# Layer kernel of a diffusion block on one core: token parts for the last two groups of the down projection, loads and splits of two earlier groups moved

## The chip, the core and the metric

One core of a Trainium2 chip runs the whole kernel. The metric is the device time in microseconds (us), the median of several executions. Engines: PE is TensorE (matrix products), DVE is VectorE, ACT is ScalarE, POOL is GpSimd, SP is SyncE, which here only issues transfers. POOL issues transfers too, on a queue of its own.

## What is computed

```python
x = x + g1 * mix
x = x + g2 * _swiglu(_modulate(_rms_norm(x, norm2_g[l]), sh2, sc2), w_ffn_in[l], w_ffn_out[l])
...
return _rms_norm(x, norm_f_g)

def _swiglu(u, w_ffn_in, w_ffn_out):
    gate, up = jnp.split(u @ w_ffn_in, 2, axis=-1)
    return (jax.nn.silu(gate) * up) @ w_ffn_out
```

There are 512 tokens (T) of 2048 features (D); the hidden layer has 5632 features. The change touches only the product with `w_ffn_out` (the down projection) and the final norm. One more number matters: the last 1024 columns of the adaptive modulation (`c @ w_ada`) is computed beside the down projection, in 16 "pieces" of 128 x 1024 weights.

## The kernel before

Every tile has features on the 128 partitions and tokens along the row. Float32 products are made of three fp32r products: high part of the weights by high part of the data, high by low, low by high. ACT makes a high part (a copy to fp32r), DVE the low part (a subtraction), and PE then multiplies.

**The down projection** has two kinds of work. The first 16 rows of 128 hidden features and all outputs are done in *the block*: eight periods (p = 64 to 71, `NALL` to `NEND` - 1) of seven products each, in the order A11, S2, S1, A22, A12, S3, S4; the count `product_done` tells how many are finished. The other 28 rows are done in *groups* of four rows: `NG` = 7 groups for each of three passes over the outputs, 21 in all, numbered gg = 0 to 20 (`LAST` = 20). Groups 0 to 6 run ahead of the block, 7 to 13 and 14 to 20 behind it. A group has one hidden tile (1 MB) and three units of weights (512 KB each; two units in the last pass). A unit is 24 matmuls of 512 tokens (L1805 to L1816), so a group of three units is 72 matmuls, one of two units 48. `SETS` gives each group one of three sets of buffers.

**Who does what for a group.** SP loads it (`group`, `hidden`, `down` in L627 to L643; buffers `hb_f` for the hidden tile and `bw_f` for a unit), waiting until the last group with the same buffers is used. ACT makes the high parts `hb_h` and `bw_h`, DVE the low parts `hb_l` and `bw_l` (`prep(gg)`: the hidden tile first, then the units in turn; PE can start once the first unit's low part is there). Each engine runs its list strictly in order, so the order written in the code decides what waits behind what.

**The pieces.** POOL loads piece n into one of four buffers, once DVE has used piece n - 4 (`pool.wait_ge(ada2_used, n - 3)`). DVE accumulates them (`late(first, end)`, L1947 and L1950, tile `ada_al`). ACT waits for the sixteenth before it splits token sums for the block (L1307), behind `prep(5)`.

**Behind the block.** POOL adds the block's results to `x1_feature_major` in device memory, two transfers a period (L799). SP waits for the last of them, then loads rows of x1 (`x1_load`), and behind them group 9.

**The end.** The last group (20) is done in two halves of 256 tokens (`half_tile`). For each half: DVE adds the result to the rows (L2685), ACT squares and scales them (L1361, L1362), PE sums squares over features with 1-column products (`mean_old` for the 12 row tiles finished earlier, `mean_new` for the last 4) and turns the last four row tiles to token order (`tail_turn`), ACT takes the root, DVE the reciprocal and scales the 1536 older columns (L2691), ACT the 512 newer (L1371), and SP stores (L723, L725). All stores are 4 MB.

Of the kernel before, what the change touches and what calls it, by code (L numbers as in the profile page):

```python
# [117 lines left out]
def build(nc, x, c, ctx_in, c_ctx, w_ada, b_ada, norm1_g, norm2_g, w_in, conv_w, conv_b, lru_wa, lru_ba,  # L118
          lru_wx, lru_bx, lru_lambda, w_lru_out, w_pool, pool_scale, w_fourier, b_gate, w_out,
          w_ffn_in, w_ffn_out, norm_f_g, consts, dft, out, x_fm):  # L120
    with ExitStack() as stack:
# [148 lines left out]
        def sem(name):  # L270
            return stack.enter_context(nc.semaphore(name))
# [64 lines left out]
        half0_done, half1_done, x2_ready = sem("half0_done"), sem("half1_done"), sem("x2_ready")  # L336
# [13 lines left out]
        def splits_before(gg):  # L350
            return 4 * gg if gg <= 2 * NG else 3 * gg + 2 * NG
# [46 lines left out]
        def _(sp):  # L398
# [293 lines left out]
            for p in range(NALL, NEND):  # L692
                ahead = p + 2 < NEND
                sp.wait_ge(product_done, p * 7 + 1)
                if ahead:
                    block_load(p + 2, "A11")
                if p == NEND - 1:
                    down(NG, 2)
                    sp.wait_ge(product_done, p * 7 + 2)
                    down(NG, 1)  # L700
                if p == NEND - 2:
                    sp.wait_ge(product_done, p * 7 + 3)
                    down(NG, 0)
                    sp.wait_ge(product_done, p * 7 + 5)
                    hidden(NG)
                for n, v in ((4, "A22"), (5, "A12"), (6, "S3")):
                    if ahead:
                        sp.wait_ge(product_done, p * 7 + n)
                        block_load(p + 2, v)
            sp.wait_ge(product_done, 7 * NEND)  # L710
            sp.wait_ge(c21_done, NEND)
            group(NG + 1)
            sp.wait_ge(s12_done, NEND)
            sp.wait_ge(gate_stored, P_STORED + 32 * ND)
            x1_load(0, 3)
# [5 lines left out]
            for t in range(4):
                sp.wait_ge(old_scaled, t + 1)
                sp.dma_start(out[0, P * t:P * t + P, 0:12 * P], out_tm[:, t, 0:12 * P]).then_inc(out_stored, 16)  # L723
                sp.wait_ge(new_scaled, t + 1)
                sp.dma_start(out[0, P * t:P * t + P, 12 * P:D], out_tm[:, t, 12 * P:D]).then_inc(out_stored, 16)  # L725
# [77 lines left out]
        def _(act):  # L803
# [549 lines left out]
                prep(gg)  # L1353

            act.activation(spare[:, :], eps_t[:, :], ACT.Sqrt)
            for h in range(2):
                cols = slice(h * TH, h * TH + TH)
                for j in range(4):
                    k = 12 + j
                    act.wait_ge(x2_ready, 4 * h + j + 1)  # L1360
                    act.activation(sqt[:, j, cols], x1b[j // 2][:, j % 2, cols], ACT.Square).then_inc(sqt_done, 1)  # L1361
                    act.activation(x_fin[j // 2][:, j % 2, cols], x1b[j // 2][:, j % 2, cols], ACT.Copy,  # L1362
                                   scale=prm[:, C_NF + k:C_NF + k + 1]).then_inc(xt_ready, 1)
                act.wait_ge(ms_ready, h + 2)
                ms = (main[:, 0, 0:2], main[:, 2, 0:2])[h]
                act.activation(rfin[:, 2 * h:2 * h + 2], ms, ACT.Sqrt, bias=eps_t[:, :], scale=1.0 / D).then_inc(rms_ready, 1)
                act.wait_ge(rfin_ready, h + 1)
                act.wait_ge(tail_turned, h + 1)
                for t in range(2):
                    src = main[:, 2 + t, :] if h == 0 else main[:, t, :]  # L1370
                    act.activation(out_tm[:, 2 * h + t, 12 * P:D], src, ACT.Copy,  # L1371
                                   scale=rfin[:, 2 * h + t:2 * h + t + 1]).then_inc(new_scaled, 1)


        @block.tensor
        def _(pe):
# [449 lines left out]
                        ins = pe.transpose(main[:, 2 + n, t * P:t * P + P], x_fin[q % 3][:, n, t * P:t * P + P], ident)  # L1826
                ins.then_inc(fin_turned, 1)

            for gg in range(LAST):
                ps, g = gg // NG, gg % NG  # L1830
                if g == 0 and ps < 2:
                    end = (NALL, NEND)[ps]
# [37 lines left out]
            last = splits_before(LAST)  # L1870

            def half_tile(h, j):

                u, n = j // 2, j % 2
                cols = slice(h * TH, h * TH + TH)
                pe.wait_ge(b_lo, last + 2 + u)
                for cc in range(UC):
                    b = SETS[LAST]
                    w_h, w_l = bw_h[3 * b + u][:, cc, n * P:n * P + P], bw_l[3 * b + u][:, cc, n * P:n * P + P]
                    dst = out_bank(u, n)[:, cols]  # L1880
# [3 lines left out]
                ins.then_inc((half0_done, half1_done)[h], 1)  # L1884

            def mean_old(dst, h):
                for n in range(2):
                    for t in range(2):
                        pe.matmul(dst[:, t:t + 1], sq2_acc[:, n, (2 * h + t) * P:(2 * h + t + 1) * P], ones[:, 0:1],
                                  start=(n == 0 and t == 0), stop=False, skip_group_check=True)  # L1890

            def mean_new(dst, h):
                for j in range(4):
                    pe.wait_ge(sqt_done, 4 * h + j + 1)
                    for t in range(2):
                        ins = pe.matmul(dst[:, t:t + 1], sqt[:, j, (2 * h + t) * P:(2 * h + t + 1) * P], ones[:, 0:1],
                                        start=False, stop=(j == 3), skip_group_check=True)
                ins.then_inc(ms_ready, 1)

            def tail_turn(h, j, dst):  # L1900
                pe.wait_ge(xt_ready, 4 * h + j + 1)
                for t in range(2):
                    ins = pe.transpose(dst[:, t, j * P:j * P + P], x_fin[j // 2][:, j % 2, (2 * h + t) * P:(2 * h + t + 1) * P], ident)
# [28 lines left out]
        def _(dve):
# [744 lines left out]

            for u in range(2):
                dve.wait_ge(rows_landed[u], 48 + (32, 48, 32)[u])
            for h in range(2):  # L2680
                cols = slice(h * TH, h * TH + TH)
                for j in range(4):
                    u, n, k = j // 2, j % 2, 12 + j
                    dve.wait_ge((half0_done, half1_done)[h], j + 1)
                    dve.scalar_tensor_tensor(x1b[u][:, n, cols], out_bank(u, n)[:, cols], mod2[:, 48 + k:49 + k], x1b[u][:, n, cols],  # L2685
                                             ALU.mult, ALU.add).then_inc(x2_ready, 1)
                dve.wait_ge(rms_ready, h + 2)
                dve.reciprocal(rfin[:, 2 * h:2 * h + 2], rfin[:, 2 * h:2 * h + 2]).then_inc(rfin_ready, 1)
                dve.wait_ge(rfin_ready, h + 1)
                for t in range(2 * h, 2 * h + 2):  # L2690
# [51 lines left out]
```

## Time and profile before

| what | us |
|---|---|
| median of 3 runs (lowest, highest) | 2627.28 (2625.63, 2630.27) |
| the profiled execution | 2632.57 |
| its span from first to last instruction | 2630.8 |
| PE busy | 2593.4 |
| DVE busy | 1988.0 |
| ACT busy | 1198.8 |

The profiled execution is one run with the recorder on. Times in its rows are microseconds from the first instruction. Busy shares overlap, since engines run beside each other; only the waits of PE and the stretch after its last product can be given back where PE is nearly always busy.

### The profile page before, as it was taken

How to read it: one execution, taken by the hardware profiler on the slowest of the kernel's cores; microseconds unless marked ns; L12 is line 12 of the kernel's file. 1: busy time of each engine (PE TensorE's matmuls, PEld its weight loads, DVE VectorE, ACT ScalarE, POOL GpSimd, SP SyncE). 2: the span in 40 equal slices, each digit the busy share in tenths (PEclk: the TensorE clock that was granted, in tenths of full speed). 3: DMA queues.
4: the chain of work that ended last, by engine and by line, in shares of the span. 5: the costliest groups of instructions: out<-in, count | busy, mean ns of one | idle time of the engine just before them, and what ended most of it. 6: DMA issues, size and time to landing. Idle time of an engine off the chain costs nothing.

```text
span 2630.8 us, 38065 instructions
## 1 busy us (share of the span) xinstructions
PE 2593.4 (99%) x14009; PEld 2201.1 (84%) x14009; DVE 1988.0 (76%) x2176; ACT 1198.8 (46%) x1377; POOL 205.8 (8%) x277
## 2 busy tenths in 40 slices
PE   7999999999999999999999999999999999999998
PEld 5688777878888888888788888888888888888787
DVE  4466898768999999775668788788787868986443
ACT  4223666354555555422344444444444435454433
POOL 0020000000001111110000010000000100011000
PEclk8999999999999999999999999999999999999999
DMA  9975433855556666896568887888887867665643
GB/s 365 368 265 182 134 126 116 292 176 160 173 155 163 164 159 148 293 328 230 141 163 200 201 203 193 208 199 197 210 202 195 206 244 246 164 131 134 245 160 144
DMA packets 528117, 524.95 MB, mean 200 GB/s; under 512 B 16473, under 2 KB 466849, under 8 KB 523297
## 3 DMA queue, kind: packets, MB, share of 16 engines
q1 hardware_dynamic: 479296, 379.96, 46.9%
q0 software_dynamic: 44176, 126.90, 20.9%
q10 hardware_dynamic: 4560, 16.95, 1.6%
q8 instruction: 56, 0.92, 0.1%
q14 instruction: 29, 0.23, 0.0%
HBM read 427.27 MB, written 54.53 MB: 183 GB/s over the span
## 4 chain that ended last, share of the span: by engine, by line
PE 92%; DVE 3%; DMA 2%; ACT 1%; issue 1%; ACTq 0%; SPq 0%; DVEq 0%; POOL 0%; POOLq 0%
PE aux L1674 17%; PE main L1674 17%; PE aux L1678 9%; PE main L1678 9%; PE main L1381 8%; PE main L1382 8%; PE main L1383 8%; PE aux L1813 2%; PE aux L1814 2%; PE aux L1815 2%; DMA bw_f<-in_w_ffn_out 1%; PE aux L1557 1%; PE aux L1433 1%; DMA ada_pc<-in_w_ada 1%; PE aux L1382 1%
## 5 line engine op out<-in xcount | busy, mean ns | idle before, releaser
L1015 ACT ACTIVATE h_S<-f_S 128x1024 fp32r<-128x1024 f32 x288 | 297.3, 1057 | 431.7 <-DVE f_S L2254 207.8
L2266 DVE TENSOR_TENSOR l_S<-f_S,h_S 128x1024 fp32r<-128x1024 f32 x288 | 344.9, 1219 | 16.9 <-ACT h_S L1015 16.9
L2266 DVE TENSOR_TENSOR l_A<-f_A,h_A 128x1024 fp32r<-128x1024 f32 x216 | 261.3, 1221 | 71.1 <-ACT h_A L1015 58.3
L1015 ACT ACTIVATE h_A<-f_A 128x1024 fp32r<-128x1024 f32 x216 | 227.5, 1057 | 145.6 <-PE aux L1678 71.9
L1674 PE MATMUL main<-t_both,h_S 128*128 128x512 f32 x864 | 216.3, 392 | 0.0
L1674 PE MATMUL aux<-t_both,h_S 128*128 128x512 f32 x864 | 216.3, 392 | 0.0
L1940 DVE TENSOR_TENSOR w_lo<-w_raw,w_hi 128x1024 fp32r<-128x1024 f32 x120 | 145.8, 1221 | 92.7 <-ACT w_hi L809 92.5
L1381 PE MATMUL main<-u_both,w_hi 128*128 128x512 f32 x512 | 211.4, 413 | 2.5 <-DVE u_both L2468 2.5
L809 ACT ACTIVATE w_hi<-w_raw 128x1024 fp32r<-128x1024 f32 x120 | 125.4, 1053 | 182.0 <-DMA w_raw<-in_w_out 63.5
L1382 PE MATMUL main<-u_both,w_hi 128*128 128x512 f32 x512 | 201.9, 394 | 0.0
L1383 PE MATMUL main<-u_both,w_lo 128*128 128x512 f32 x512 | 201.0, 393 | 0.0
L1674 PEld LDWEIGHTS aux<-t_both,h_S 128*128 128x128 f32 x864 | 155.4, 189 | 27.8
L1674 PEld LDWEIGHTS main<-t_both,h_S 128*128 128x128 f32 x864 | 155.4, 189 | 27.8
L1674 PE MATMUL main<-u_both,h_A 128*128 128x512 f32 x576 | 144.2, 392 | 0.0
L1674 PE MATMUL aux<-u_both,h_A 128*128 128x512 f32 x576 | 144.1, 392 | 0.0
L1813 PE MATMUL aux<-hb_h,bw_h 128*128 128x512 f32 x320 | 126.0, 394 | 3.2 <-DVE bw_l L2564 3.2
L1814 PE MATMUL aux<-hb_l,bw_h 128*128 128x512 f32 x320 | 125.3, 392 | 0.0
L1815 PE MATMUL aux<-hb_h,bw_l 128*128 128x512 f32 x320 | 125.1, 391 | 0.0
L1678 PEld LDWEIGHTS main<-t_both,l_S 128*128 128x128 f32 x864 | 117.9, 190 | 8.4
L1678 PEld LDWEIGHTS aux<-t_both,l_S 128*128 128x128 f32 x864 | 117.9, 190 | 8.4
L1381 PEld LDWEIGHTS main<-u_both,w_hi 128*128 128x128 f32 x512 | 97.6, 191 | 30.8 <-issue 14.6
L1678 PE MATMUL aux<-t_both,l_S 128*128 128x256 f32 x864 | 120.5, 282 | 0.0
(331 smaller groups left out, 5470.4 us busy)
## 6 DMA issues: line engine op xcount, KB each, us to landing
f_A<-in_w_ffn_in SPq DMA_DIRECT2D x120, 512.0 KB, 5.3
f_S<-in_w_ffn_in SPq DMA_DIRECT2D x80, 512.0 KB, 4.1
f_S<-f_A POOLq DMA_DIRECT2D x80, 512.0 KB, 5.6
f_A<-in_w_in SPq DMA_DIRECT2D x72, 512.0 KB, 3.8
bw_f<-in_w_ffn_out SPq DMA_DIRECT2D x56, 512.0 KB, 7.3
w_raw<-in_w_in SPq DMA_DIRECT2D x48, 512.0 KB, 3.7
ada_pc<-in_w_ada SPq DMA_DIRECT2D x48, 512.0 KB, 7.5
ada_pw<-in_w_ada POOLq DMA_DIRECT2D x48, 512.0 KB, 6.3
```

The lines of the kernel that those rows point to most:

```text
L809: act.activation(w_hi[:, u % RING], w_raw[:, u % RING], ACT.Copy).then_inc(hi_done, 1)
L1015: act.activation(wh[v][:, :, :], wf[b][v][:, :, :], ACT.Copy).then_inc(w_hi_done, 1)
L1381: pe.matmul(dst, wh, m_hi_ap, start=start, stop=False, skip_group_check=shared)
L1382: pe.matmul(dst, wh, m_lo_ap, start=False, stop=False, skip_group_check=shared)
L1383: return pe.matmul(dst, wl, m_hi_ap, start=False, stop=stop, skip_group_check=shared)
L1674: pe.matmul(dst.rearrange("p (s n) -> p s n", n=TH), wh[v][:, k, :], moving[v](k)[0], start=start and k == 0, stop=False, skip_group_check ...
L1678: ins = pe.matmul(dst[:, low * TH:low * TH + TH], wl[b][v][:, k, :], moving[v](k)[1], start=False, stop=k == HK - 1, skip_group_check=True)
L1813: pe.matmul(dst, w_h, hb_h[b][:, cc, :], start=start and cc == 0, stop=False, skip_group_check=again)
L1814: pe.matmul(dst, w_h, hb_l[b][:, cc, :], start=False, stop=False, skip_group_check=again)
L1815: ins = pe.matmul(dst, w_l, hb_h[b][:, cc, :], start=False, stop=stop and cc == UC - 1, skip_group_check=again)
L1940: dve.tensor_tensor(w_lo[:, s], w_raw[:, s], w_hi[:, s].bitcast(F32), ALU.subtract).then_inc(lo_done, 1)
L2266: dve.tensor_tensor(wl[b][v][:, :, :], wf[b][v][:, :, :], wh[v][:, :, :].bitcast(F32), ALU.subtract).then_inc(w_lo_done, 1)
```

## The change

Three edits. (1) SP loads two weight units of group 8 during the block's last period, and its hidden tile and third unit ahead of the last product and not behind it. (2) DVE makes the low parts of group 4 ahead of pieces 8, 9 and 10, and not behind them. (3) The last two groups are computed in token parts. Group 19 comes in two halves of 256 tokens, group 20 in parts of 256, 128 and 128 tokens; the order on PE is: 19 first half, 20 first part, 19 second half, 20 second part, 20 third part. `mean_old` for all tokens stands ahead of group 19. Each part has its own root and scaling, and its rows are stored on their own, the older columns of a part ahead of its newer ones.

```diff
+PARTS = ((0, 2), (2, 1), (3, 1))
...
                     sp.wait_ge(product_done, p * 7 + 2)
                     down(NG, 1)
+                    for n, u in ((4, 2), (5, 0)):
+                        sp.wait_ge(product_done, p * 7 + n)
+                        down(NG + 1, u)
...
-            sp.wait_ge(product_done, 7 * NEND)
+            sp.wait_ge(product_done, 7 * NEND - 1)
             sp.wait_ge(c21_done, NEND)
-            group(NG + 1)
+            hidden(NG + 1)
+            down(NG + 1, 1)
...
             block_token_sums()
-            late(8, 11)
             prep(4)
-            late(11, 16)
+            late(8, 16)
             prep(5)
...
-            for gg in range(LAST):
+            for gg in range(LAST - 1):
...
+            mean_old()
             for j in range(4):
-                half_tile(0, j)
...
+                tile_part(LAST - 1, j, *PARTS[0])
+            for j in range(4):
+                last_tile(0, j)
+            for j in range(4):
+                pe.wait_ge(x2_ready, j + 1)
+                tile_part(LAST - 1, j, 2, 2)
+                if j == 1:
+                    mean_new(0)
...
             for j in range(4):
-                ins = tail_turn(0, j, main[:, 2:4, :])
+                ins = tail_turn(0, j)
             ins.then_inc(tail_turned, 1)
...
+            for j in range(4):
+                last_tile(1, j)
+            for j in range(2):
+                last_tile(2, j)
+            mean_new(1)
+            for j in range(2, 4):
+                last_tile(2, j)
+            for j in range(4):
+                ins = tail_turn(1, j)
+            ins.then_inc(tail_turned, 1)
             for j in range(3):
-                tail_turn(1, j, main[:, 0:2, :])
-            mean_new(main[:, 2, 0:2], 1)
-            tail_turn(1, 3, main[:, 0:2, :]).then_inc(tail_turned, 1)
+                tail_turn(2, j)
+            mean_new(2)
+            tail_turn(2, 3).then_inc(tail_turned, 1)
...
+            add_rows(0)
+            scale_old(0)
+            add_rows(1)
+            add_rows(2)
+            scale_old(1)
+            scale_old(2)
```

`tile_part(gg, j, first, n)` is the old `half_tile` with the group and the tokens as arguments: 12 matmuls of n x 128 tokens for the j-th output tile. `add_rows(r)` holds the four additions of a part, `scale_old(r)` its reciprocal and the scaling of its older columns.

On DVE, between the sums of token halves for the block (`t_f`) and the low parts of group 5 (`hb_l0`, `bw_l0`), the program before has:

```order
881 L2596 TENSOR_TENSOR t_f_81<-u_f_53,t_f_81 128x2048
882 L1950 SCALAR_TENSOR_TENSOR ada2_al_198<-ada2_pl_197,cvec_205,ada2_al_198 128x1024 x3
883 L2559 TENSOR_TENSOR hb_l1_131<-hb_f1_130,hb_h1_132 128x2048
884 L2564 TENSOR_TENSOR bw_l3_146<-bw_f3_145,bw_h3_147 128x1024
885 L2564 TENSOR_TENSOR bw_l4_149<-bw_f4_148,bw_h4_150 128x1024
886 L2564 TENSOR_TENSOR bw_l5_152<-bw_f5_151,bw_h5_153 128x1024
887 L1950 SCALAR_TENSOR_TENSOR ada2_al_198<-ada2_pl_197,cvec_205,ada2_al_198 128x1024 x5
888 L2559 TENSOR_TENSOR hb_l0_128<-hb_f0_127,hb_h0_129 128x2048
```

and the changed one, where the three pieces stand behind the four rows of group 4 (`hb_l1` to `bw_l5`) and join the other five:

```order
881 L2636 TENSOR_TENSOR t_f_81<-u_f_53,t_f_81 128x2048
882 L2599 TENSOR_TENSOR hb_l1_131<-hb_f1_130,hb_h1_132 128x2048
883 L2604 TENSOR_TENSOR bw_l3_146<-bw_f3_145,bw_h3_147 128x1024
884 L2604 TENSOR_TENSOR bw_l4_149<-bw_f4_148,bw_h4_150 128x1024
885 L2604 TENSOR_TENSOR bw_l5_152<-bw_f5_151,bw_h5_153 128x1024
886 L1990 SCALAR_TENSOR_TENSOR ada2_al_198<-ada2_pl_197,cvec_205,ada2_al_198 128x1024 x8
887 L2599 TENSOR_TENSOR hb_l0_128<-hb_f0_127,hb_h0_129 128x2048
```

So eight pieces in a row now stand between the low parts of group 4 and those of group 5.

At the very end of PE's list, the program before has the last matmuls of the second half (256 tokens), then sums (`ones,sqt`) and turns (`const,x_fin`):

```order
4516 L1881 MATMUL aux<-hb_h_132,bw_h_150 128x256
4517 L1882 MATMUL aux<-hb_l_131,bw_h_150 128x256
4518 L1883 MATMUL aux<-hb_h_132,bw_l_149 128x256
4519 L1889 MATMUL main<-ones,sq_acc 128x1 x4
4520 L1903 MATMUL main<-const,x_fin_168 128x128 x4
4521 L1903 MATMUL main<-const,x_fin_169 128x128 x2
4522 L1896 MATMUL main<-ones,sqt 128x1 x8
4523 L1903 MATMUL main<-const,x_fin_169 128x128 x2
```

The changed one ends with the third part (128 tokens), the turns of part two, and then those of part three:

```order
4613 L1903 MATMUL aux<-hb_h_132,bw_h_150 128x128
4614 L1904 MATMUL aux<-hb_l_131,bw_h_150 128x128
4615 L1905 MATMUL aux<-hb_h_132,bw_l_149 128x128
4616 L1937 MATMUL main<-const,x_fin_168 128x128 x2
4617 L1937 MATMUL main<-const,x_fin_169 128x128 x2
4618 L1937 MATMUL aux<-const,x_fin_168 128x128 x2
4619 L1937 MATMUL aux<-const,x_fin_169 128x128
4620 L1928 MATMUL main<-ones,sqt 128x1 x4
4621 L1937 MATMUL aux<-const,x_fin_169 128x128
```

The products over the last 256 tokens are twice as many and half as wide, and the sums over older rows (`sq_acc`) no longer stand here.

## Rows read from the trace of the kernel before

**Rows 1.** Page, first part: busy time, share of the span, instructions.
```profile
PE 2593.4 (99%) x14009; PEld 2201.1 (84%) x14009; DVE 1988.0 (76%) x2176; ACT 1198.8 (46%) x1377; POOL 205.8 (8%) x277
```

**Rows 2.** Timeline of PE: start, duration, instruction, [idle before it and its releaser].
```profile
2206.79 0.50 PE L1813 MATMUL aux<-hb_h,bw_h 128*128 128x512 f32 x1 [1.12 <-DVE bw_l L2564]
...
2449.96 0.50 PE L1813 MATMUL aux<-hb_h,bw_h 128*128 128x512 f32 x1 [2.11 <-DVE bw_l L2564]
```

**Rows 3.** Timeline of DVE around groups 4 and 5.
```profile
2172.55 1.28 DVE L1950 SCALAR_TENSOR_TENSOR ada_al<-ada_pl,cvec,ada_al 128x1024 f32<-128x1024 f32 x1 [2.48 <-DMA ada_pl<-in_w_ada]
...
2199.34 4.06 DVE L1950 SCALAR_TENSOR_TENSOR ada_al<-ada_pl,cvec,ada_al 128x1024 f32<-128x1024 f32 x3
2203.32 2.28 DVE L2559 TENSOR_TENSOR hb_l<-hb_f,hb_h 128x2048 fp32r<-128x2048 f32 x1
2205.52 3.49 DVE L2564 TENSOR_TENSOR bw_l<-bw_f,bw_h 128x1024 fp32r<-128x1024 f32 x3
...
2218.43 1.29 DVE L1950 SCALAR_TENSOR_TENSOR ada_al<-ada_pl,cvec,ada_al 128x1024 f32<-128x1024 f32 x1 [4.06 <-DMA ada_pl<-in_w_ada]
2219.63 2.29 DVE L2559 TENSOR_TENSOR hb_l<-hb_f,hb_h 128x2048 fp32r<-128x2048 f32 x1
```

**Rows 4.** Timeline of ACT: the high part of group 4's hidden tile.
```profile
2197.76 1.92 ACT L1256 ACTIVATE hb_h<-hb_f 128x2048 fp32r<-128x2048 f32 x1 [12.80 <-DMA hb_f<-hidden_feature_major]
```

**Rows 5.** Timeline of POOL: loads of pieces 12 and 15, a block transfer.
```profile
2200.93 0.54 POOL L734 DMA_DIRECT2D ada_pl<-in_w_ada  x1 [9.66 <-DVE ada_al L1950]
...
2210.70 0.53 POOL L734 DMA_DIRECT2D ada_pl<-in_w_ada  x1 [6.47 <-DVE ada_al L1950]
...
2403.89 1.20 POOL L799 DMA_DIRECT2D x_feature_major<-u_hi_spare  x1 [3.75 <-issue]
```

**Rows 6.** Timeline of SP: group 5's hidden tile, the last rows' first store.
```profile
2205.70 0.34 SPq L631 DMA_DIRECT2D hb_f<-hidden_feature_major  x1
...
2623.41 0.33 SPq L723 DMA_DIRECT2D out_x<-out_tm  x1
```

**Rows 7.** Windows of 2 us: engines' busy time, PE clock, DMA share, GB/s.
```profile
2204.00:2206.00 2.00, 1.67 (x8) 1.06 (x6) 2.00 (x2) 2.00 (x3) 0.23 (x1) 1.00 0.84 250
2216.00:2218.00 2.00, 2.00 (x10) 1.68 (x9) 0.00 (x0) 0.82 (x1) 0.00 (x0) 1.00 0.42 149
```

**Rows 8.** Windows behind two idle stretches of PE, same columns.
```profile
2450.00:2456.00 6.00, 6.00 (x19) 4.81 (x20) 6.00 (x5) 6.00 (x6) 0.00 (x0) 0.72 1.06 380
1268.00:1276.00 8.00, 7.62 (x22) 6.17 (x23) 8.00 (x12) 4.80 (x7) 0.00 (x0) 0.63 0.01 2
```

**Rows 9.** Chain that ended last, from the block's end to group 9.
```profile
2418.18 1.18 POOL x_feature_major L799
...
2426.66 4.65 DMA x_feature_major<-u_hi_spare
2431.37 0.34 SPq L655
```

**Rows 10.** Timeline of PE: group 19, group 20 and the last sums.
```profile
2592.27 0.39 PE L1813 MATMUL aux<-hb_h,bw_h 128*128 128x512 f32 x1
...
2603.15 0.28 PE L1881 MATMUL aux<-hb_h,bw_h 128*128 128x256 f32 x1
...
2610.34 0.95 PE L1889 MATMUL main<-ones,sq_acc 128*128 128x1 f32 x8
...
2612.67 1.84 PE L1896 MATMUL main<-ones,sqt 128*128 128x1 f32 x16
2614.38 1.07 PE L1903 MATMUL main<-const,x_fin 128*128 128x128 f32 x8
2615.20 0.36 PE L1881 MATMUL aux<-hb_h,bw_h 128*128 128x256 f32 x1
...
2618.15 0.95 PE L1889 MATMUL main<-ones,sq_acc 128*128 128x1 f32 x8
```

**Rows 11.** Timeline of PE: a plain f32 product of 256 columns.
```profile
234.77 0.59 PE L1556 MATMUL aux<-xcv,gate_w 128*128 128x256 f32 x2
```

More of the change, by code:

```diff
@@ L719, in _ @@
                 group(gg)
[L721 to L725, printed above, removed]
+            for first, n in PARTS:
+                for t in range(first, first + n):
+                    sp.wait_ge(old_scaled, t + 1)
+                    sp.dma_start(out[0, P * t:P * t + P, 0:12 * P], out_tm[:, t, 0:12 * P]).then_inc(out_stored, 16)
+                for t in range(first, first + n):
+                    sp.wait_ge(new_scaled, t + 1)
+                    sp.dma_start(out[0, P * t:P * t + P, 12 * P:D], out_tm[:, t, 12 * P:D]).then_inc(out_stored, 16)
             sp.wait_ge(out_stored, 128)
@@ new lines, in new_rows, with part_root @@
+            def new_rows(r, j):
+                cols = slice(PARTS[r][0] * P, sum(PARTS[r]) * P)
+                act.wait_ge(x2_ready, 4 * r + j + 1)
+                act.activation(sqt[:, j, cols], x1b[j // 2][:, j % 2, cols], ACT.Square).then_inc(sqt_done, 1)
+                act.activation(x_fin[j // 2][:, j % 2, cols], x1b[j // 2][:, j % 2, cols], ACT.Copy,
+                               scale=prm[:, C_NF + 12 + j:C_NF + 13 + j]).then_inc(xt_ready, 1)
+            def part_root(r):
+                act.wait_ge(ms_ready, r + 2)
+                first, n = PARTS[r]
+                act.activation(rfin[:, first:first + n], main[:, 0, first:first + n], ACT.Sqrt, bias=eps_t[:, :], scale=1.0 / D).then_inc(rms_ready, 1)
@@ new lines, in part_out @@
+            def part_out(r):
+                act.wait_ge(rfin_ready, r + 1)
+                act.wait_ge(tail_turned, r + 1)
+                first, n = PARTS[r]
+                for t in range(first, first + n):
+                    act.activation(out_tm[:, t, 12 * P:D], (main[:, 2, :], main[:, 3, :], main[:, 1, :], aux[:, 0, :])[t], ACT.Copy,
+                                   scale=rfin[:, t:t + 1]).then_inc(new_scaled, 1)
+            for j in range(4):
+                new_rows(0, j)
+            part_root(0)
@@ L1867, in _, with tile_part @@
                         period(p, p % 2)
[L1870 to L1876, printed above, removed]
+            def tile_part(gg, j, first, n):
+                u, half = j // 2, j % 2
+                cols = slice(first * P, (first + n) * P)
+                pe.wait_ge(b_lo, splits_before(gg) + 2 + u)
                 for cc in range(UC):
[L1878 to L1880 removed]
+                    b = SETS[gg]
+                    w_h, w_l = (w[3 * b + u][:, cc, half * P:half * P + P] for w in (bw_h, bw_l))
+                    dst = out_bank(u, half)[:, cols]
                     pe.matmul(dst, w_h, hb_h[b][:, cc, cols], start=False, stop=False, skip_group_check=True)
@@ L1887, in mean_old, with mean_new @@
                 for n in range(2):
-                    for t in range(2):
-                        pe.matmul(dst[:, t:t + 1], sq2_acc[:, n, (2 * h + t) * P:(2 * h + t + 1) * P], ones[:, 0:1],
+                    for t in range(4):
+                        pe.matmul(main[:, 0, t:t + 1], sq2_acc[:, n, t * P:(t + 1) * P], ones[:, 0:1],
                                   start=(n == 0 and t == 0), stop=False, skip_group_check=True)
-            def mean_new(dst, h):
+            def mean_new(r):
+                first, n = PARTS[r]
+                if r:
+                    pe.wait_ge(rms_ready, r + 1)
@@ L1893, in mean_new @@
                 for j in range(4):
-                    pe.wait_ge(sqt_done, 4 * h + j + 1)
-                    for t in range(2):
-                        ins = pe.matmul(dst[:, t:t + 1], sqt[:, j, (2 * h + t) * P:(2 * h + t + 1) * P], ones[:, 0:1],
+                    pe.wait_ge(sqt_done, 4 * r + j + 1)
+                    for t in range(first, first + n):
+                        ins = pe.matmul(main[:, 0, t:t + 1], sqt[:, j, t * P:(t + 1) * P], ones[:, 0:1],
                                         start=False, stop=(j == 3), skip_group_check=True)
@@ L1898, in mean_new, with tail_turn @@
                 ins.then_inc(ms_ready, 1)
[L1900 to L1903, printed above, removed]
+            def tail_turn(r, j):
+                first, n = PARTS[r]
+                pe.wait_ge(xt_ready, 4 * r + j + 1)
+                for t in range(first, first + n):
+                    bank = (main[:, 2, :], main[:, 3, :], main[:, 1, :], aux[:, 0, :])[t]
+                    ins = pe.transpose(bank[:, j * P:j * P + P], x_fin[j // 2][:, j % 2, t * P:(t + 1) * P], ident)
```

69 lines of the change are left out of this document (30 added, 39 removed).

## The prediction

> **What bounds the kernel.** I read the page first: PE is busy 99% of the span [rows 1], so time comes from PE's few waits, from its clock, from added PE work, and from what lies behind its last product. Then the waits and the timeline of PE. In the stretches that the change touches it waits twice, both times for DVE's low part of a weight unit: 1.12 us at 2206.79, the start of group 4, and 2.11 us at 2449.96, the start of group 9 [rows 2]. Then DVE, ACT, POOL and SP around the two waits, the windows for the traffic, and last PE's row by row from group 19 on.
>
> **Edit 1, group 8's loads.** Who holds group 9? SP loads x1 and group 9 only when POOL's last transfer of block results has landed (2426.66 + 4.65 = 2431.3, then 2431.37) [rows 9]. POOL issued that transfer 8.48 us behind the one before it (2418.18) [rows 9]; a period earlier the same pair stood 3.75 + 1.2 = 4.9 us apart [rows 5]. The second is issued when the first has landed, it seems, and this first one lands amid group 8's 2.6 MB, which SP issues right behind the block's last product. In the changed kernel 1 MB of it is gone by then and the rest starts about 0.6 us earlier, so I expect the usual 4.9 us: x1 and group 9 come 3.5 us sooner. Group 9's first low part, ready at 2449.9, would be there at 2446.4, and PE wants it at 2449.96 - 2.11 = 2447.85. The wait of 2.1 us goes. So does what the clock took behind it: from 2450 to 2456 PE was granted 0.72 of full speed [rows 8], a mean of its two levels, 1.2 and 2.4 GHz; 6 x 0.28 = 1.7 us. Gain 3.8 us; nothing if the pair stays 8.5 us apart. The two units loaded inside the block fill buffers whose products are over.
>
> **Edit 2, group 4's low parts.** The gain is plain. ACT has the hidden tile's high part at 2199.68 [rows 4], DVE is kept by three pieces until 2203.32 [rows 3]. Without them `hb_l` starts at about 2199.7, and the first unit is ready 2.20 + 1.2 us later [rows 3], at 2203.1, ahead of PE's 2206.79 - 1.12 = 2205.67. Gain 1.1 us.
>
> What is late next? The three pieces give back the buffers for pieces 12 to 14. Before, POOL issued piece 12 at 2200.93, 0.3 us behind the use of piece 8 [rows 3, 5]. Now piece 8 comes behind group 4's four subtractions (2.20 + 3.49, so at about 2205.4), is used up at 2206.7, and pieces 12 to 15 are issued at 2207.0, 2208.4, 2209.8 and 2211.1, one per 1.35 us of DVE [rows 3]. Group 5's 2.6 MB are issued at 2205.70 as before [rows 6]. Before, the transfer engines moved about 250 GB/s of pieces from 2202.5 to 2207.3 [rows 7] and went quiet at 2216.8 (0.42 of the window from 2216) [rows 7]; DVE got piece 15 at 2218.43, 1.6 us behind, 7.7 us from its issue [rows 3, 5]. Those 4.8 us x 250 GB/s = 1.2 MB now have to move later. Group 5 and piece 15, 3.15 MB, took the 9.5 us to 2216.8, 330 GB/s, so 1.2 MB are 3.6 us; I take 3.4. Piece 15 lands at 2221.8. That SP's traffic does not let pieces pass is seen earlier: with SP's loads queued, one piece of 0.5 MB came each 2.48 + 1.28 = 3.76 us [rows 3].
>
> Behind piece 15 DVE needs 1.2 us to `hb_l` and 3.4 us to the first unit of group 5 [rows 3]: 2226.4. PE is done with group 4 at 2205.67 + 72 x 0.227 = 2222.0 (0.227 us is group 19's 10.88 us over 48 matmuls [rows 10]). So a new wait of 4.5 us stands at group 5. Before, PE began group 5 at 2206.8 + 16.4 = 2223.2; now at 2226.5, 3.3 us later with the gain of 1.1 counted in. The clock: behind the wait of 2.11 us it cost 1.7 us, behind the longer idle stretch at 1264 to 1268 it was 0.63 over 8 us, 2.9 us [rows 8]. I take 2.7. Edit 2 costs 6.0 us; from both sides: a gain of 1.1 if there is no wait, a cost of 7 if the 1.2 MB move at 250 GB/s. ACT's split of token sums, prep(6) and the block's weights on DVE shift by the same 3 to 4 us as PE and stay ahead of it.
>
> **Edit 3, the end.** I count from group 19's start, 2592.27; the span ended 38.5 us later. Prices: a matmul of 512 tokens 0.227 us, of 256 tokens 7.19 us / 60 = 0.120, eight turns 0.82, `mean_new` for two token tiles 1.71 (16 records), so 0.107 a record [rows 10]. Group 19 in halves: 96 x 0.12 for 48 x 0.227, +0.6 us.
>
> A fp32r matmul of 128 tokens runs nowhere in this trace. From below: the 128-column turns take 0.82 / 8 = 0.103 and the 1-column records 0.107 [rows 10], so narrower than 256 buys almost nothing; each has its own weights to load. From above: a plain f32 product of 256 columns lasts 0.59 us over two records where fp32r's lasts 0.28 [rows 10, 11], that is 0.43 against 0.12 of stream, and half of that for 128 columns is 0.215. I take 0.107, since the turns carry one 128-column pass with one weight load, as these would. The 96 matmuls of parts two and three are 10.3 us for the 5.8 us of 48 wider ones: +4.5.
>
> The Trainium skill speaks otherwise here. "TensorE: Matmul & The Clock Gate", section "Back-to-back issue gap", gives about 81 ns for a matmul of 128 columns in a stream; by it edit 3 would cost 2.5 us less than my sum. The trace's 0.103 and 0.107 stand against it.
>
> In order: `mean_old` 1.7 (16 records), three rounds of 48 matmuls 17.3, `mean_new` 1.7, eight turns 0.8, 10.3 for the parts, `mean_new` of part two 0.85: the last product ends at 32.6 (before: 2618.15, 25.9). The addition of a narrow tile, 0.6 us, then reciprocal and one scaling, 1.25 us, put SP's store of token tile 2 at 34.45. Before it was 2623.41, 31.14 [rows 6]. Behind it stood 7.4 us to the end of the span, moving 2 MB. The changed order still scales tile 2 only behind the last addition, so the same 2 MB go out in one burst behind it: end at 41.8. Edit 3 costs 3.3 us. What it gains, the later sums and root of part three hidden under tile 2's store, is in that number (3.4 us less behind the last product); the cover is the transfer.
>
> **Sum.** -3.8 + 6.0 + 3.3 = +5.5 us. The profiled execution took 2632.57 for a span of 2630.8, so 2638.1 with it; it lies 5.3 us above the median, and on the median 2627.28 + 5.5 = 2632.8. A measurement of this kernel tells about 0.2%, 5.3 us, from no change: the forecast is slower by a hair.
>
> **Rivals.**
> A. Narrow fp32r matmuls stream at the plain f32 rate, 0.215 us. For it: no fp32r product here is narrower than 256 columns, even where 128 would be handy. Against: the turns. It adds 96 x 0.108 = 10.4 us to whatever else holds, 2643.2 with edit 2 as forecast, 2636 with rival B.
> B. The other side: piece 15 is in time. If its flag is there by 2222.0 - 3.4 - 1.2 = 2217.4, 6.3 us from its issue, group 5 has no wait and edit 2 gains its 1.1 us. It would need POOL's queue to pass SP's; the 3.76 us a piece and the 7.7 us of piece 15 speak against it. Time: 2627.28 - 3.8 - 1.1 + 3.3 = 2625.7, no change. If piece 15 takes the old 7.7 us it lands at 2218.8: a wait of 1.4 us, near the 1.12 us of [rows 2], and 2627.
> C. Edit 1 gains nothing, because POOL's pair stays apart for a reason of its own: 2636.6.
>
> **How the numbers follow.** Narrow matmuls at 0.107 and a long wait at group 5, my forecast: 0.42, its own range 2630.5 to 2635. The same matmuls with B: 0.2. Rival A with either: 0.3. C: 0.08 (it needs narrow matmuls at 0.107 as well). The range runs from B, 2625, to A with the long wait, 2644. Slower by over 0.2% (above 2632.5): all of A, 0.3, C, and 0.18 of my own case, which the line cuts near its middle: 0.56. Within: the other 0.24 of it and most of B, 0.38. Faster is the part of B in which narrow matmuls also take near 0.07 us: 0.06.
>
> **What would show it.** Edit 1: POOL's last two block transfers about 5 us apart, no wait at group 9 and the clock at 1.00 behind it. Edit 2: no wait at group 4, a wait of 3 to 5.5 us at group 5, behind a DVE that idles for pieces 12 to 15, then some 5 us with the clock at half. Edit 3: starts 0.107 us apart among the 128-token matmuls (0.215 under A), the store of tile 2 about 3.3 us later behind group 19's start than before, and 7.4 us from it to the end. The prediction is wrong if group 5 starts without a wait, if the narrow matmuls are not near 0.107, or if tile 2's rows leave ahead of the last product.

## The result

The changed kernel takes 2634.99 us (median of 16 runs, 2630.76 to 2637.45), the kernel before 2629.2 us in the same session (16 runs, 2625.63 to 2634.36): ratio 1.0021, 95% interval 1.0014 to 1.0028. The forecast was 2632.8 us on a base of 2627.28, a ratio of 1.0021. It is slower by a hair, as forecast, but two of the three terms were off by 1.4 and 2.4 us in opposite directions.

The span of the profiled execution grew from 2630.8 to 2633.1 us. Cut at PE's own milestones, with the start of a group read as the start of its first product, it divides like this. Group 19's start in the kernel after, and in every run that has the new tail, is the start of the sums (`mean_old`, 1.7 us) that now stand ahead of its first product; so both tails hold the same work.

| stretch | before | after | difference |
|---|---|---|---|
| start to group 4's first product | 2206.79 | 2203.57 | -3.22: 1.28 between group 3's last product and group 4's first, where the wait was; 1.94 in code that is the same |
| group 4's start to group 5's | 16.46 | 19.60 | +3.14 |
| group 5's start to the block's | 34.50 | 36.23 | +1.73 |
| the block | 156.40 | 156.40 | 0 |
| block's end to group 9's start | 35.81 | 33.46 | -2.35 |
| group 9's start to group 19's | 142.31 | 140.65 | -1.66 |
| group 19's start to the end | 38.53 | 43.19 | +4.66 |

So edit 1 gives 4.0 us (-2.35 and -1.66), edit 2 costs 3.6 (-1.28, +3.14, +1.73), edit 3 costs 4.7. The 1.94 us of the untouched part are one execution against another and belong to no edit; without them the sum is +4.2. The medians differ by 5.8: the profiled execution of the kernel before was 3.4 us above its median (2632.57 for 2629.2), that of the kernel after 0.1 below it. So 1.5 us of the 5.8 stay unaccounted for.

**PE's waits and starts.** The list of PE's waits of the kernel after has one for a low part, where the kernel before had two [rows 2]:

```profile
PE aux L1837 <- DVE bw_l L2604: 3.1, 1, 3.1
```

The timeline of PE of the kernel after at groups 5 and 9, with the wait in brackets:

```profile
2223.17 0.52 PE L1837 MATMUL aux<-hb_h,bw_h 128*128 128x512 f32 x1 [3.13 <-DVE bw_l L2604]
...
2449.26 0.48 PE L1837 MATMUL aux<-hb_h,bw_h 128*128 128x512 f32 x1
```

Group 9 starts with no bracket, and so does group 4: both old waits are gone, and a new one of 3.13 us stands at group 5.

**What DVE does ahead of it.** DVE's timeline of the kernel after answers to [rows 3]:

```profile
2203.98 5.45 DVE L1990 SCALAR_TENSOR_TENSOR ada_al<-ada_pl,cvec,ada_al 128x1024 f32<-128x1024 f32 x4
...
2212.30 1.28 DVE L1990 SCALAR_TENSOR_TENSOR ada_al<-ada_pl,cvec,ada_al 128x1024 f32<-128x1024 f32 x1 [2.87 <-DMA ada_pl<-in_w_ada]
2215.08 1.28 DVE L1990 SCALAR_TENSOR_TENSOR ada_al<-ada_pl,cvec,ada_al 128x1024 f32<-128x1024 f32 x1 [1.50 <-DMA ada_pl<-in_w_ada]
2216.76 1.28 DVE L1990 SCALAR_TENSOR_TENSOR ada_al<-ada_pl,cvec,ada_al 128x1024 f32<-128x1024 f32 x1 [0.40 <-DMA ada_pl<-in_w_ada]
2218.50 1.29 DVE L1990 SCALAR_TENSOR_TENSOR ada_al<-ada_pl,cvec,ada_al 128x1024 f32<-128x1024 f32 x1 [0.45 <-DMA ada_pl<-in_w_ada]
2219.70 2.28 DVE L2599 TENSOR_TENSOR hb_l<-hb_f,hb_h 128x2048 fp32r<-128x2048 f32 x1
```

DVE is done with piece 11 at 2209.4 and then waits for each of pieces 12 to 15. Piece 15 is used at 2218.50. POOL's timeline of the kernel after has the issues of pieces 12 and 15, and the last pair of block transfers:

```profile
2205.57 0.54 POOL L741 DMA_DIRECT2D ada_pl<-in_w_ada  x1 [16.05 <-DVE ada_al L1990]
...
2209.92 0.53 POOL L741 DMA_DIRECT2D ada_pl<-in_w_ada  x1 [1.06 <-DVE ada_al L1990]
...
2419.82 1.18 POOL L806 DMA_DIRECT2D x_feature_major<-u_hi_spare  x1 [13.44 <-ACT u_hi_spare L1048]
2424.57 1.20 POOL L806 DMA_DIRECT2D x_feature_major<-u_hi_spare  x1 [3.56 <-issue]
```

Piece 15 is used 8.6 us behind its issue (2218.50 - 2209.92). The pair of block transfers now stands 4.75 us apart, for 8.48 in [rows 9].

**Traffic and clock.** The last three columns of a window are PE's clock, the share of the transfer engines and GB/s. Of the kernel before, [rows 7] lacks those in between:

```profile
2206.00:2208.00 2.00, 1.21 (x5) 1.04 (x6) 2.00 (x3) 2.00 (x3) 0.00 (x0) 1.00 0.90 326
...
2210.00:2212.00 2.00, 2.00 (x11) 1.65 (x10) 1.79 (x3) 1.43 (x1) 0.53 (x1) 1.00 0.92 308
...
2214.00:2216.00 2.00, 2.00 (x11) 1.65 (x10) 0.37 (x1) 1.63 (x2) 0.00 (x0) 1.00 1.12 400
```

The kernel after:

```profile
2206.00:2208.00 2.00, 2.00 (x10) 1.65 (x10) 1.90 (x2) 2.00 (x2) 0.63 (x2) 1.00 0.94 379
...
2214.00:2216.00 2.00, 2.00 (x10) 1.69 (x9) 0.92 (x1) 0.00 (x0) 0.00 (x0) 1.00 1.05 404
2216.00:2218.00 2.00, 2.00 (x10) 1.65 (x9) 1.60 (x2) 1.06 (x1) 0.00 (x0) 1.00 0.67 230
...
2222.00:2224.00 2.00, 0.83 (x3) 0.69 (x4) 2.00 (x2) 2.00 (x3) 0.00 (x0) 0.88 0.97 402
2224.00:2226.00 2.00, 2.00 (x6) 1.57 (x5) 2.00 (x3) 2.00 (x2) 0.00 (x0) 0.50 1.01 357
2226.00:2228.00 2.00, 2.00 (x8) 1.58 (x7) 2.00 (x2) 2.00 (x2) 0.00 (x0) 0.77 1.10 353
...
2450.00:2456.00 6.00, 6.00 (x28) 4.93 (x27) 6.00 (x5) 3.47 (x4) 0.00 (x0) 1.00 0.99 352
```

From 2206 to 2216 the transfers move 379 to 404 GB/s (mean 391; before 308 to 400, mean 347), and the engines go quiet 0.67 of the way through the window from 2216, at 2217.3. Behind the new wait the clock is at half (0.50) for a while: 2 x (0.12 + 0.50 + 0.23) = 1.7 us. Behind group 9, where it was 0.72 [rows 8], it is 1.00.

**The end.** PE's timeline of the kernel after from group 19's first sums on:

```profile
2589.91 1.84 PE L1918 MATMUL main<-ones,sq_acc 128*128 128x1 f32 x16
...
2611.55 0.31 PE L1903 MATMUL aux<-hb_h,bw_h 128*128 128x128 f32 x1
...
2619.62 1.00 PE L1928 MATMUL main<-ones,sqt 128*128 128x1 f32 x8
...
2622.86 0.38 PE L1903 MATMUL aux<-hb_h,bw_h 128*128 128x128 f32 x1
...
2624.98 1.71 PE L1928 MATMUL main<-ones,sqt 128*128 128x1 f32 x8
```

SP's stores of tiles 2 and 3 in the same timeline (L729 is the old part of a tile's rows, L732 the new one):

```profile
2625.22 0.33 SPq L729 DMA_DIRECT2D out_x<-out_tm  x1
2627.59 0.33 SPq L732 DMA_DIRECT2D out_x<-out_tm  x1
2628.26 0.33 SPq L729 DMA_DIRECT2D out_x<-out_tm  x1
2628.64 0.46 SPq L732 DMA_DIRECT2D out_x<-out_tm  x1
```

And the windows of that stretch:

```profile
2620.00:2622.00 2.00, 2.00 (x20) 2.00 (x19) 0.17 (x1) 0.75 (x3) 0.00 (x0) 1.00 0.00 0
2622.00:2624.00 2.00, 2.00 (x16) 2.00 (x15) 0.64 (x3) 0.60 (x2) 0.00 (x0) 0.72 0.00 0
2624.00:2626.00 2.00, 2.00 (x12) 2.00 (x10) 1.15 (x3) 0.60 (x2) 0.00 (x0) 0.50 0.00 0
2626.00:2628.00 2.00, 1.00 (x5) 0.70 (x4) 0.95 (x2) 1.28 (x3) 0.00 (x0) 0.50 0.96 393
```

Seventy-two 128-token matmuls fill 2611.55 to 2619.62: 8.07 us, 0.112 each. From about 2622.9 the clock is at half although PE has been busy for 2.00 of every 2 us; the last sums take 1.71 us for 1.00 before. Tile 2's store is issued 35.3 us behind group 19's start (2589.91), tile 3's 38.35, and the span ends at 43.19.

### The profile page after: what moved, and what is told of

Same layout as the page of the kernel before. It is cut to its first block and busy times, and to the rows that moved or that the text cites. A ratio compares the mean times of both kernels' runs of the same rounds, so it can differ in the third digit from the quotient of the medians.

```text
span 2633.1 us, 38280 instructions
## 1 busy us (share of the span) xinstructions
PE 2596.6 (99%) x14105; PEld 2206.8 (84%) x14105; DVE 1989.4 (76%) x2181; ACT 1200.0 (46%) x1386; POOL 205.5 (8%) x277
## 5 line engine op out<-in xcount | busy, mean ns | idle before, releaser
L1405 PEld LDWEIGHTS main<-u_both,w_hi 128*128 128x128 f32 x512 | 97.2, 190 | 30.6 <-issue 14.5
L1837 PE MATMUL aux<-hb_h,bw_h 128*128 128x512 f32 x304 | 119.6, 393 | 3.1 <-DVE bw_l L2604 3.1
L1702 PE MATMUL main<-t_both,l_S 128*128 128x256 f32 x864 | 120.5, 282 | 0.0
L1698 PEld LDWEIGHTS aux<-u_both,h_A 128*128 128x128 f32 x576 | 103.8, 189 | 18.7
```

The source lines that it names most:

```text
L1405: pe.matmul(dst, wh, m_hi_ap, start=start, stop=False, skip_group_check=shared)
L1698: pe.matmul(dst.rearrange("p (s n) -> p s n", n=TH), wh[v][:, k, :], moving[v](k)[0], start=start and k == 0, stop=False, skip_group_check ...
L1702: ins = pe.matmul(dst[:, low * TH:low * TH + TH], wl[b][v][:, k, :], moving[v](k)[1], start=False, stop=k == HK - 1, skip_group_check=True)
L1837: pe.matmul(dst, w_h, hb_h[b][:, cc, :], start=start and cc == 0, stop=False, skip_group_check=again)
```

## The experiments

Theory at the outset: the three edits act each in its own stretch and add up, and each term has the mechanism that the prediction gave it. Rivals: they interact, or a term stands for something else (pieces late by their own issue and not by shared traffic; a tail that is long because of its order and not of its narrow parts). A tenth of a per cent is 2.6 us.

**First run: edit 1 alone**, the kernel before with only SP's order for group 8:

```diff
                     down(NG, 1)
+                    for n, u in ((4, 2), (5, 0)):
+                        sp.wait_ge(product_done, p * 7 + n)
+                        down(NG + 1, u)
...
-            sp.wait_ge(product_done, 7 * NEND)
+            sp.wait_ge(product_done, 7 * NEND - 1)
             sp.wait_ge(c21_done, NEND)
-            group(NG + 1)
+            hidden(NG + 1)
+            down(NG + 1, 1)
```

> The kernel before with the loads of group 8 inside the block and nothing else. My theory: POOL's last two block transfers stand about 5 us apart, SP loads group 9 some 2.5 to 3.5 us earlier, the wait at group 9 (2.1 us) and the half-speed stretch behind it (1.7 us) are gone, 4.0 us less in all, ratio 0.9985. The wait of about 1.1 us at group 4 stays. Rival (POOL's pair is apart for a reason of its own): 8.5 us apart still, the wait at group 9 stays, ratio 1.000.

Measured: 2626.78 us, ratio 0.999 (0.9981 to 0.9999). POOL's timeline of this run:

```profile
2416.37 1.18 POOL L803 DMA_DIRECT2D x_feature_major<-u_hi_spare  x1 [12.98 <-ACT u_hi_spare L1045]
2421.22 1.20 POOL L803 DMA_DIRECT2D x_feature_major<-u_hi_spare  x1 [3.67 <-issue]
```

The pair stands 4.85 us apart, group 9 starts with no wait, and the clock is 1.00 from 2446 to 2456. With the second run, in which the pair is 8.44 us apart and the wait at group 9 2.17 us, that is the prediction's chain with its cause switched on and off. The landings bear it out: of the last four block transfers the slowest took 8.2 us from issue to landing in the kernel before and in the second run, 5.2 in this one and 5.3 in the kernel after. Which part of edit 1 does it, the 1 MB loaded early or the earlier start of the rest, was not told apart.

**Second run: edit 2 alone.**

```diff
-            late(8, 11)
             prep(4)
-            late(11, 16)
+            late(8, 16)
             prep(5)
```

> The kernel before with the low parts of group 4 ahead of pieces 8 to 10 and nothing else. My theory: no wait at group 4, pieces 12 to 15 are issued 5 to 6 us later, DVE idles for them, group 5 starts 3 us or more late and the clock is at half for 3 to 4 us behind it: 3.6 us more (1.1 to 1.3 gained, 3.1 waited, 1.7 by the clock), ratio 1.0014. The wait and the half-speed stretch at group 9 stay as before. Rival (group 5 is late by a hazard of one execution, the order of the list is harmless): 1.1 us less, ratio 0.9996, no wait at group 5.

Measured: 2633.63 us, ratio 1.0014 (1.0005 to 1.0023). PE's timeline of this run has the two waits:

```profile
2222.54 0.50 PE L1813 MATMUL aux<-hb_h,bw_h 128*128 128x512 f32 x1 [3.06 <-DVE bw_l L2564]
...
2451.05 0.50 PE L1813 MATMUL aux<-hb_h,bw_h 128*128 128x512 f32 x1 [2.17 <-DVE bw_l L2564]
```

The long wait at group 5 comes with edit 2 (the first run, which has not got it, waits 0.23 us there, the third not at all); the one at group 9 is that of before. The clock was 0.79 over the 8 us from 2222, 1.7 us.

**Third run: edit 3 alone**, that is the table of parts and all that reads it, with the old order ahead of it.

```diff
+PARTS = ((0, 2), (2, 1), (3, 1))
```

> The kernel before with the last two groups in token parts and nothing else. My theory: from group 19's start to the end of the span 43 us in place of 38.5, 3.3 (as forecast) to 4.7 us more (as the changed kernel's trace has it), ratio 1.0013 to 1.0018. 128-token matmuls start 0.112 us apart. The waits at groups 4 and 9 stay as before. Rival (the parts pay for themselves, and the loss seen is all of edit 2's): ratio 1.000 or less.

Measured: 2635.5 us, ratio 1.0018 (1.0009 to 1.0027). SP's timeline of this run:

```profile
2622.80 0.33 SPq L725 DMA_DIRECT2D out_x<-out_tm  x1
2623.73 0.33 SPq L728 DMA_DIRECT2D out_x<-out_tm  x1
2624.41 0.63 SPq L725 DMA_DIRECT2D out_x<-out_tm  x1
```

Group 19 starts at 2587.81 and the span is 2630.2. Tile 2's store comes 35.0 us behind that start, 7.4 us before the end, and the whole stretch is 42.4. In this execution the clock stays at 1.00 until PE is done, and the end is one burst of 2 MB behind tile 2's store, as the prediction has it. The product of the three ratios is 0.999 x 1.0014 x 1.0018 = 1.0022, against 1.0021 for all three: the edits add up, as far as ratios that are each known to 0.0009 can tell.

**Fourth run: edit 1 and a finer split.** Group 4's low parts ahead of the pieces as in edit 2, but group 5's hidden tile and first unit ahead of pieces 13 to 15:

```diff
-            late(8, 16)
-            prep(5)
+            late(8, 13)
+            hidden_lo(5)
+            down_lo(5, 0)
+            late(13, 16)
+            down_lo(5, 1)
+            down_lo(5, 2)
```

> The kernel before with edit 1, the low parts of group 4 ahead of the pieces as in edit 2, and group 5's hidden tile and first weight unit made between pieces 12 and 13 and not behind piece 15. My theory (group 5 is late because its low parts stand behind pieces whose transfers come late): no wait at group 4, none at group 5, none at group 9, 1.2 + 4.0 = 5.2 us less, ratio 0.998. Rival (group 5 is late because its own transfers come late): a wait of 2 us or more stays at group 5, ratio 0.999 to 1.000.

Measured: 2624.81 us, ratio 0.9984 (0.9975 to 0.9993), the fastest of all. DVE's timeline of this run:

```profile
2211.85 1.28 DVE L1954 SCALAR_TENSOR_TENSOR ada_al<-ada_pl,cvec,ada_al 128x1024 f32<-128x1024 f32 x1 [3.58 <-DMA ada_pl<-in_w_ada]
2213.05 2.28 DVE L2563 TENSOR_TENSOR hb_l<-hb_f,hb_h 128x2048 fp32r<-128x2048 f32 x1
2215.25 1.22 DVE L2568 TENSOR_TENSOR bw_l<-bw_f,bw_h 128x1024 fp32r<-128x1024 f32 x1
2216.39 4.05 DVE L1954 SCALAR_TENSOR_TENSOR ada_al<-ada_pl,cvec,ada_al 128x1024 f32<-128x1024 f32 x3
```

DVE works on group 5 while pieces 13 to 15 travel, and then takes the three without a wait. Group 5 starts at 2219.28 with no wait; groups 4 and 9 have none either. The loss of edit 2 is thus the one place of `prep(5)` behind piece 15. The ratio fell short of the 0.998 expected, but its interval takes that in.

**Fifth run: two parts of 256 tokens**, the changed kernel with

```diff
-PARTS = ((0, 2), (2, 1), (3, 1))
+PARTS = ((0, 2), (2, 2))
```

and without the turns, sums and rows of a third part.

> The changed kernel with its last group cut into two parts of 256 tokens, in place of 256, 128 and 128; the rest of the new order stays (tiles in rounds per part, group 19 in two parts, edits 1 and 2 as they are). Theory (the loss of edit 3 lies in the two 128-token parts: 0.112 us for half a tile's matmul instead of about 0.12 for a whole one, and a third round of root, rows and stores): the stretch from group 19's first product to the end falls from 43.2 to 38.3 us or so, the clock stays at 1.00 until the last product, and the whole comes to the time of the kernel before plus what edits 1 and 2 sum to (-4.0 + 3.6), ratio 1.0000 with bounds 0.9990 and 1.0008. Rival (the loss lies in the order of the rounds, a turn of group 19's rows between the products, or in the split of group 19): the stretch stays above 41 us and the ratio at 1.0015 or more.

Measured: 2630.95 us, ratio 1.0005 (0.9996 to 1.0014). From group 19's start (2589.11) to the end (2628.0) it is 38.9 us, for 38.5 before and 43.2 with three parts. The new order of rounds and group 19 in halves cost 0.4 us; the 128-token parts cost the rest. It is also the control for the other two edits: -4.0 + 3.6 + 0.4 = 0.0, inside the interval.

**Sixth run: tile 2's rows first.** The changed kernel with tile 2's turns, scaling and stores ahead of the last two column tiles of tile 3's part. For PE:

```diff
             for j in range(2):
                 last_tile(2, j)
             mean_new(1)
-            for j in range(2, 4):
-                last_tile(2, j)
             for j in range(4):
                 ins = tail_turn(1, j)
             ins.then_inc(tail_turned, 1)
+            for j in range(2, 4):
+                last_tile(2, j)
```

and the same on ACT and DVE.

> The changed kernel with tile 2's scaling, turning and rows moved ahead of the last two column tiles of tile 3's part. Theory A (the prediction's: the end follows the last burst, 7.4 us from tile 2's store): tile 2's store is issued 1 to 2.6 us earlier, and the end with it, ratio against the kernel before 1.0012 to 1.0018. Theory B (tile 3's own chain, its last product, root, rows and store, sets the end, since the profile after has a gap in the transfers between tile 2's stores and tile 3's): tile 2's stores come earlier and the end moves by less than 0.4 us, or is later by the turns that now lie ahead of the last products (up to 0.5 us), ratio 1.0020 to 1.0023.

Measured: 2633.29 us, ratio 1.0011 (1.0002 to 1.0020). SP's timeline of this run:

```profile
2622.54 0.33 SPq L729 DMA_DIRECT2D out_x<-out_tm  x1
...
2626.80 0.33 SPq L729 DMA_DIRECT2D out_x<-out_tm  x1
```

Counted from group 19's start (2590.22), tile 2's store is at 32.3 for 35.0 in the third run, tile 3's at 36.6 in both, the end (2631.5) at 41.3 for 42.4. The clock was 1.00 through the last product in both. So with the clock kept the end does follow tile 2's burst, theory A, but only for the first 1.1 us of the 2.7 by which the store came earlier; then tile 3's own chain, 4.7 us from its store to the end, is the bound. The transfer engines are idle between the two bursts (8 GB/s or less from 2626.0 to 2627.5).

**Seventh run: the split order and two parts of 256.**

> Edit 1, the finer split order of group 5's low parts that the fourth run had, and the last group in two parts of 256 tokens. Theory (the three are independent, as the first three runs were): -4.0 of edit 1 and about -1.3 of the split, and the tail of the fifth run, so 0.9984 if that tail is as long as before (38.5 us), 0.9982 if it is 0.5 us shorter. Rival (the 256-token parts cost as well): tail over 39.5 us, ratio 0.9988 or more.

Measured: 2625.49 us, ratio 0.9985 (0.9976 to 0.9994); the tail is 38.9 us again (2584.79 to 2623.7). It beats both kernels, but not the fourth run: even in its cheap form, edit 3 brings nothing that these runs can tell.

**Eighth run: the split order with all three parts.** The diff is that of the fourth run, on the changed kernel.

> The changed kernel, all three edits, with group 5's low parts split among pieces 13 to 15 as in the fourth run. Theory (edit 2 costs 3.6 us by its place and the split gives back that and 1.3 more, edit 3's tail costs 3.9 to 4.7 us whatever stands ahead of it): no wait at group 5, the stretch from group 19's first product to the end 42.4 us with the clock at 1.00 through the last product or 43.2 with a fall, and the sum -4.0 - 1.3 + 4.3, ratio 0.9996 with bounds 0.9993 and 1.0004. Rival (the tail was long because of what stood ahead of it): tail under 41 us, ratio 0.999 or less.

Measured: 2630.86 us, ratio 1.0003 (0.9993 to 1.0012). No wait at group 5, and a tail of 44.8 us (2584.32 to 2629.1), longer than the two cases that I had allowed. Windows of this run:

```profile
2614.00:2616.00 2.00, 2.00 (x18) 2.00 (x18) 0.35 (x1) 0.75 (x3) 0.00 (x0) 0.88 0.04 8
2616.00:2618.00 2.00, 2.00 (x12) 2.00 (x11) 0.35 (x1) 0.45 (x2) 0.00 (x0) 0.50 0.00 0
```

The clock fell already at about 2615.5, 31 us behind group 19's start, again with PE busy throughout. -4.0 - 1.3 + 6.3 = +1.0 us is 1.0004, for 1.0003 measured. That what stood ahead of it made the tail long is out.

**Ninth run: group 5's last two units held back.** The changed kernel with a wait on SP:

```diff
                 for u in range(UNITS[gg]):
+                    if (gg, u) == (5, 1):
+                        sp.wait_ge(ada2_used, 127)
                     down(gg, u)
```

> The changed kernel with SP holding back the last two weight units of group 5 (1 MB) until piece 14 is used. Theory A (piece 15 is late because its 0.5 MB and the pieces ahead of it share the transfer engines with group 5's 2.6 MB): with 1 MB less ahead of it piece 15 is used up to 2.6 us earlier (1 MB at 390 GB/s), the wait at group 5 falls from 3.1 us to between 0.5 and 2.1, the two units land in time, and the ratio falls from 1.0021 to between 1.0008 and 1.0016. Theory B (pieces 12 to 15 are late by their own issue, one per use of a buffer, or by the queue that they stand in): the pieces keep their times, the wait stays at 3 us, ratio 1.0019 or more.

Measured: 2631.07 us, ratio 1.0006 (0.9997 to 1.0015). PE's timeline of this run at group 5:

```profile
2220.92 0.50 PE L1839 MATMUL aux<-hb_h,bw_h 128*128 128x512 f32 x1 [1.46 <-DVE bw_l L2606]
```

DVE's:

```profile
2210.88 2.67 DVE L1992 SCALAR_TENSOR_TENSOR ada_al<-ada_pl,cvec,ada_al 128x1024 f32<-128x1024 f32 x2 [2.15 <-DMA ada_pl<-in_w_ada]
2214.85 2.67 DVE L1992 SCALAR_TENSOR_TENSOR ada_al<-ada_pl,cvec,ada_al 128x1024 f32<-128x1024 f32 x2 [1.29 <-DMA ada_pl<-in_w_ada]
2217.45 2.28 DVE L2601 TENSOR_TENSOR hb_l<-hb_f,hb_h 128x2048 fp32r<-128x2048 f32 x1
```

POOL issues piece 15 at 2209.22, and DVE is done with it at 2217.45, 8.2 us later, for 9.8 in the kernel after (2219.70 - 2209.92). DVE took pieces 14 and 15 in one go from 2214.85, so piece 15 had landed by 2216.2, 7.0 us behind its issue. The wait at group 5 falls from 3.13 to 1.46 us, inside the range of theory A, and the clock behind it stays at 1.00. The ratio lies a little below theory A's 1.0008, which its interval takes in. SP's traffic is what makes the pieces late; theory B is out.

## Why the prediction was right, and where its terms were off

**Edit 1: right in mechanism and size.** -4.0 us for -3.8: the pair at 4.75 us for the 4.9 expected, no wait at group 9, the clock at 1.00. The first run alone shows it; its ratio, 2.6 us, is smaller but its interval takes in the 4. One reason for a smaller mean is visible: in the third run, which has not got edit 1, the pair stood 7.78 us apart, the wait at group 9 was 1.53 us and the clock stayed at 1.00, so what edit 1 removes is not the same in each execution. Rival C is out.

**Edit 2: right in mechanism, its size too large** (3.6 us measured, 6.0 forecast; 1.0014 for it alone). The gain of 1.1 came, as 1.28. The step that was mis-sized is "Those 4.8 us x 250 GB/s = 1.2 MB now have to move later", at 330 GB/s, which gave 3.4 us. It comes out otherwise when both kernels are counted from the same event, SP's issue of group 5:

| from SP's issue of group 5 | before | after | forecast |
|---|---|---|---|
| engines quiet, us | 11.1 (2205.70 to 2216.84) | 13.6 (2203.76 to 2217.34) | 14.5 |
| moved until then, MB | 3.8 (338 GB/s) | 4.7 (346 GB/s) | 1.2 more than before |
| DVE starts piece 15, us | 12.7 | 14.7 | 16.1 |

So 0.9 MB moved later, not 1.2: the 4.8 us ran 1.6 us past that issue, into a stretch in which the engines are at work in both kernels. (250 GB/s is the rate of one window; over the 4.8 us the trace has 286.) The 0.9 MB cost 2.4 us, and DVE then started piece 15 only 1.2 us behind the quiet, for 1.6 before. So piece 15 came 2.0 us later than before, not 3.4, and that is the main part of the 1.4 us by which the wait came out shorter (3.13 for 4.5). The rate of 330 was not exact either, since from 2206 to 2216 the queues moved 347 GB/s before and 391 after; the engines' share was 1.00 and 1.03, so the difference is not idle time, and its cause stays open. The rest of the error is the clock: 2.7 us taken from between two rows, 1.7 measured behind waits of 3.13 and 3.06 us, the same as behind the 2.11 us of [rows 2]. A longer wait did not cost more clock here. That SP's traffic holds the pieces back is shown by the ninth run, and that `prep(5)` behind piece 15 is the whole of the loss by the fourth. Rival B is out: the wait is there.

**Edit 3: right in mechanism, its size too small** (4.7 us in the profile, 3.9 with the clock kept, 3.3 forecast; 1.0018 for it alone). The step "I take 0.107" gave 0.112 at full clock: 96 x 0.005 = 0.5 us, and tile 2's store came at 35.0 for 34.45 in the third run, with 7.4 us behind it as forecast. What stands behind the last product shrank from 12.6 us to 9.1, 3.5 for the 3.4 forecast. Rival A at 0.215 is out. The Trainium skill's 81 ns ("TensorE: Matmul & The Clock Gate", "Back-to-back issue gap") does not hold for these fp32r products with a weight load each: 72 of them took 0.112 us each.

The step "the same 2 MB go out in one burst behind it" holds when the clock does (third run: 2622.80 + 7.4 = 2630.2, the span). The sixth run bears it out in part: with tile 2's rows 2.7 us earlier the end came 1.1 us earlier, until tile 3's chain bound it. In the profile of the kernel after it fails: the clock falls at about 2622.9, the last products, turns and sums run at half speed, tile 3's store slips from 36.6 to 38.35 us, behind the end of tile 2's burst, and the end from 42.4 to 43.2. This the prediction did not have at all; it looked for the clock behind waits alone. Two other profiles with three parts show it too, at a price of 1.4 us (ninth run, 43.75) and 2.4 us (eighth, 44.8), for 0.8 in the kernel after. That the narrow parts, and not the order, are the cause of the long tail is shown by the fifth run (38.9).

That the total came out at 1.0021 as forecast is partly luck: edit 2 was forecast 2.4 us too dear and edit 3 1.4 too cheap.

## What to carry to other kernels

Before you cut the output finer, price the narrower products: here one of 256 tokens took 0.120 us and one of 128 took 0.112, so the last halving nearly doubled that work (10.8 us for 5.8) for 3.5 us of sums and scaling that it could hide. When a split is moved ahead of a consumer of streamed pieces, look for what the late pieces hold back; here the cure was to put the next group's first splits among the pieces (fourth run, 0.9984), or in part to hold back the competing transfer (ninth, 1.0006), not to choose one of the two orders. And size the delay of a transfer by the bytes that move behind an event which both orders share (here SP's issue of group 5: 3.8 MB and 4.7 MB), not by a rate times a stretch that reaches across it.

## What the runs showed of the hardware that was not expected

TensorE's granted clock fell to half, its lower level of 1.2 GHz, in the middle of back-to-back 128-token fp32r products, without a wait ahead of it. It happened in three of the five profiles with 128-token parts, at about 31, 32.3 and 33 us behind group 19's start (eighth, ninth run and the kernel after), in all with PE busy for 2.00 of 2 us around the fall; in the third and sixth run the clock stayed at 1.00 to the last product. In none of the profiles with parts of 256 tokens (before, first, second, fourth, fifth, seventh) did it fall ahead of the last products. The fall stands 0.6, 1.7 and 2.4 us behind the end of part two's sums, which stand at this place in all five. What makes it fall in one execution and not in another stays open.

The clock behind PE's short waits differed too. Behind 1.46 and 1.53 us (ninth run, third run) it stayed at 1.00. Behind waits of 2.11 us (the kernel before), 2.17 and 3.06 (second run), 3.13 (the kernel after, fifth run) and 3.54 (sixth run) it fell for a few microseconds, and the price was 1.7 us each time, whatever the length within this range. The longer idle stretch ahead of the second window of [rows 8] cost more, 8 x 0.37 = 3.0 us; there the clock was at 0.50 from 1264 to 1268, before PE went on.
